# A combine of expert results with a gather buffer for every row set and a scale ahead, and one norm, summed by token tile, in the place of two

## The chip, the cores and the metric

One Trainium2 chip, one of its cores. The metric is the device time of one execution of the kernel in microseconds (us), the median of several runs. "The clock" is the granted clock of TensorE, as a share of 2.4 GHz.

## The reference

Two transformer blocks run one behind the other on 1024 tokens of 1024 features, all in float32. The first ends in a mixture of experts: every token goes to two of 16 experts and gets the weighted sum of the two results, added to the residual stream h. Between the blocks stand two norms, one behind the other:

```python
def hierarchical_moe(...):
    ...
    out = jnp.einsum('nef,efd->nd', act, w_down)
...
        h = h + hierarchical_moe(rms_norm(h, norm_ffn_g[layer]), ...)
    return rms_norm(h, norm_final_g)
...
def rmsnorm(x, g):
    xf = x.astype(jnp.float32)
    y = xf * lax.rsqrt(jnp.mean(xf * xf, axis=-1, keepdims=True) + EPS)
    return y.astype(x.dtype) * g
```

The output of `rms_norm(h, norm_final_g)` is the second block's residual stream x; its first step is `rmsnorm(x, attn_norm_2)`, whose result is multiplied with the input projections of three mixers (gated linear attention, S5, RG-LRU). Behind them come the output projection and a convolutional feed-forward part.

## The kernel before, in words

The stream h lies in SBUF with the features on the partitions: `hT` is eight pages of 128 features x 1024 tokens (`Hp[t]`). `W` ("work" in the profile) is 37 more pages of this size (`Wp[t]`; the last eight are `Bp[t]`). PSUM is used as four slots of 128x1024 that go round: every PSUM result has a number from `take()`, lies in slot number % 4, and TensorE waits in `slot(n)` until the result four numbers before it has been read (`emptied`). `done(n)` is the count of `mm_done` at which result n is complete. Each engine's program is written out by hand, and the engines meet by semaphores; there is no planner. `link()` on DVE makes the next instruction wait for the one before.

The stretch that the change touches stands between the expert blocks and the second block's projections:

- **Gathers.** The expert results lie in DRAM (`y_slots`), one row of 1024 floats for each slot. For each of the eight token tiles (128 tokens) POOL issues two indirect DMAs (L525), one for each of a token's two experts, into four buffers `YG` that go round; from the third tile on it first waits until the tile two before has been added to h (`ysum_ready`).
- **Combine.** DVE multiplies the first row set by its weight (L1593), and adds the second one times its weight (L1595). TensorE transposes the sum, 128x128 eight times (L788). DVE adds that to the tile's 128 columns in all eight pages of `hT` (L1599), before it turns to the next tile.
- **Norm `n_fin1`** (gain norm_final) and **norm `n_att2`** (gain attn_norm). One norm is: ACT squares the eight pages (L964), DVE adds them up (L1233, seven additions), TensorE sums over partitions with eight products of one column (L630) so that each token's sum lies on a partition, ACT takes the root (L971), DVE the inverse (L1239) and lays it on diagonals (L1240), TensorE spreads these with a product by ones (L639), and DVE applies gain and inverse root to each page (L1251). The first norm writes `hT` itself; its application is interleaved with the second norm's squares and additions. The second norm writes `Bp`.
- **Behind it.** `first_pair` (L590) multiplies two projections at a time, page by page as they come from the second norm; the others follow as `column_tile` (L570). DVE prepares the S5 matrices, `s5_b` and `s5_c`, which POOL has loaded once h is complete (DVE L1609 to L1620), and then waits for ACT to move the first projection out of PSUM (L1110) before it starts the RG-LRU convolution (L1626). The S5 part (L1644 and on) is a loop of eight groups on DVE, POOL and TensorE.

Names in the profile: `ps` is PSUM, `cst` holds constants, gains, the identity and the ones matrix.

## Time and profile before

| | |
|---|---|
| time of three runs | 2861.59, 2864.77, 2866.13 us; median 2864.77 |
| the profiled execution's own time | 2861.46 us |
| its span, first to last instruction | 2859.6 us |
| mean granted clock | 0.917 |
| busy, TensorE (PE) / DVE / ACT / POOL | 2511.2 / 1079.4 / 572.5 / 680.8 us |

The profile is a page of one execution with a trace of its instructions behind it, which can be asked for views. PE is TensorE's matmul side and PEld its weight loads, DVE is VectorE, ACT ScalarE, POOL GpSimd. A line "L788 MATMUL" is what line 788 of the kernel issued. A timeline row has the start, the length, engine, line, operation, output<-input, shape and count, and in brackets how long the engine was idle before it and what released it. A float32 product appears as two matmul instructions, a transpose as one. A windows row has, for a stretch of the span, its length, the busy time of PE, PEld, DVE, ACT and POOL with the instructions in brackets (only PE where so asked), the granted clock, the DMA share and GB/s. Averages over the whole span say little here: the stretch of the change is some 100 us long and is read by itself.

### The profile page before, as it was taken

How to read it: one execution, taken by the hardware profiler on the slowest of the kernel's cores; microseconds unless marked ns; L12 is line 12 of the kernel's file. 1: busy time of each engine (PE TensorE's matmuls, PEld its weight loads, DVE VectorE, ACT ScalarE, POOL GpSimd, SP SyncE). 2: the span in 40 equal slices, each digit the busy share in tenths (PEclk: the TensorE clock that was granted, in tenths of full speed). 3: DMA queues.
4: the chain of work that ended last, by engine and by line, in shares of the span. 5: the costliest groups of instructions: out<-in, count | busy, mean ns of one | idle time of the engine just before them, and what ended most of it. 6: DMA issues, size and time to landing. Idle time of an engine off the chain costs nothing. (4 is left out here: it accounts for less than half of the span.)

```text
span 2859.6 us, 27595 instructions
## 1 busy us (share of the span) xinstructions
PE 2511.2 (88%) x11034; PEld 1824.4 (64%) x11034; DVE 1079.4 (38%) x1788; ACT 572.5 (20%) x758; POOL 680.8 (24%) x448
## 2 busy tenths in 40 slices
PE   5999999997974999972896665989989999999997
PEld 4888899997762444432342224675458888888885
DVE  6400244454322111125589992552142212222124
ACT  3101455665101111102210000220021101001011
POOL 2323443462202000001023331000003233232321
PEclk9999999998976999995898887866989999999998
DMA  3111222233125677223000000000111111111111
GB/s 134 45 52 37 64 66 79 78 104 129 37 96 198 264 269 311 90 89 106 23 30 22 15 15 15 8 8 8 37 45 46 43 59 41 48 52 44 52 33 70
DMA packets 72044, 211.90 MB, mean 74 GB/s; under 512 B 4912, under 2 KB 36656, under 8 KB 68976
## 3 DMA queue, kind: packets, MB, share of 16 engines
q1 hardware_dynamic: 55712, 141.19, 14.3%
q0 software_dynamic: 11744, 52.70, 5.3%
q10 hardware_dynamic: 4464, 16.25, 1.4%
q8 instruction: 91, 1.49, 0.2%
q14 instruction: 33, 0.27, 0.0%
HBM read 165.03 MB, written 45.09 MB: 73 GB/s over the span
## 5 line engine op out<-in xcount | busy, mean ns | idle before, releaser
L608 PE MATMUL ps<-work_part 128*128 128x512 f32 x1472 | 574.3, 390 | 9.0 <-POOL work_part L463 7.2
L610 PE MATMUL ps<-work_part 128*128 128x512 f32 x1472 | 573.5, 390 | 0.0
L609 PE MATMUL ps<-work_part 128*128 128x512 f32 x1120 | 436.3, 390 | 0.0
L461 POOL CAST work_part<-ring 128x1024 fp32r<-128x1024 f32 (+2 forms) x108 | 104.9, 971 | 1147.1 <-PE ps L610 644.1
L608 PEld LDWEIGHTS ps<-work_part 128*128 128x128 f32 x1472 | 276.7, 188 | 67.7 <-issue 8.4
L610 PEld LDWEIGHTS ps<-work_part 128*128 128x128 f32 x1472 | 276.6, 188 | 57.7
L570 PE MATMUL ps<-work,ring 128*128 128x512 f32 x640 | 278.1, 595 | 2.7 <-DVE work L1790 2.7
L463 POOL TENSOR_TENSOR work_part<-ring,work_part 128x1024 fp32r<-128x1024 f32 (+2 forms) x108 | 241.1, 2233 | 8.6
L609 PEld LDWEIGHTS ps<-work_part 128*128 128x128 f32 x1120 | 210.6, 188 | 43.8
L570 PEld LDWEIGHTS ps<-work,ring 128*128 128x128 f32 x640 | 122.0, 191 | 157.4 <-issue 153.1
L759 PE MATMUL ps<-work 128*128 x496 | 218.6, 594 | 0.7 <-SPq L414 0.4
L1435 DVE CUSTOM_DVE_ANT_0 hT<-ps,hT 128x1024 f32<-128x1024 f32 (+2 forms) x86 | 85.1, 991 | 337.7 <-PE ps L674 337.7
L692 PE MATMUL ps<-work,hT 128*128 128x64 f32 x1600 | 194.8, 272 | 1.8 <-DVE work L1446 1.5
L692 PEld LDWEIGHTS ps<-work,hT 128*128 128x128 f32 x1600 | 188.5, 192 | 3.8 <-issue 1.9
L1464 DVE TENSOR_TENSOR hT<-ps,hT 128x1024 f32<-128x1024 f32 x48 | 58.8, 1225 | 341.8 <-PE ps L610 239.2
L759 PEld LDWEIGHTS ps<-work 128*128 128x128 f32 x496 | 92.1, 191 | 105.3 <-issue 105.3
L609 PE MATMUL ps<-hT_part,work_part 128*128 128x512 f32 x352 | 136.9, 389 | 0.0
L674 PE MATMUL ps<-work_part 128*128 128x512 f32 (+1 forms) x448 | 125.0, 396 | 1.6 <-ACT work L1007 1.1
L630 PE MATMUL ps<-cst,work 128*128 128x1 f32 x224 | 43.4, 324 | 81.0 <-DVE work L1233 81.0
L775 PE MATMUL ps<-work 128*128 x248 | 111.6, 592 | 1.6 <-DVE work L1575 1.6
L964 ACT ACTIVATE work<-hT 128x1024 f32<-128x1024 f32 x48 | 50.4, 1058 | 306.2 <-DVE hT L1464 222.2
L1569 DVE TENSOR_TENSOR work<-ps,work 128x256 f32<-128x256 f32 x31 | 13.2, 425 | 243.6 <-ACT work L1071 243.6
(271 smaller groups left out, 3210.7 us busy)
## 6 DMA issues: line engine op xcount, KB each, us to landing
work<-w_moe SPq DMA_DIRECT2D x16, 3072.0 KB, 11.2
ring<-w_up_units SPq DMA_DIRECT2D x44, 512.0 KB, 3.2
ring<-w_in_units SPq DMA_DIRECT2D x42, 512.0 KB, 3.3
x_slots<-hT SPq DMA_DIRECT2D x31, 512.0 KB, 3.5
work<-x_slots POOLq DMA_DIRECT2D x31, 512.0 KB, 4.3
y_slots<-work ACTq DMA_DIRECT2D x31, 512.0 KB, 2.6
ring<-w_down_units SPq DMA_DIRECT2D x24, 384.0 KB, 3.1
ring<-w_out_units SPq DMA_DIRECT2D x16, 512.0 KB, 3.3
```

The lines of the kernel that those rows point to most:

```text
L461: pool.tensor_copy(WHI[n % 2][:, 0:cols], w).then_inc(whi_ready, 1)
L463: pool.tensor_tensor(WLO[n % 2][:, 0:cols], w, WHI_F[n % 2][:, 0:cols], ALU.subtract).then_inc(wlo_ready, 1)
L570: mm = pe.matmul(ps[:, half * HALF:(half + 1) * HALF], w[:, k * P:(k + 1) * P], rhs[k][:, half * HALF:(half + 1) * HALF], start=(k == 0), ...
L608: pe.matmul(ps[:, c], whi[:, w], hi[k][:, c], start=(k == 0), stop=False)
L609: pe.matmul(ps[:, c], whi[:, w], lo[k][:, c], start=False, stop=False)
L610: mm = pe.matmul(ps[:, c], wlo[:, w], hi[k][:, c], start=False, stop=(k == len(hi) - 1))
L674: mm = pe.matmul(ps[:, b * HALF:b * HALF + w], QS[h % 2][:, i * P:(i + 1) * P], part[h % 2][:, c0:c0 + w], start=(part is KH), stop=(part ...
L692: mm = pe.matmul(ps[:, 0:DH], PT[u % 2][:, j * P:(j + 1) * P], Wp[16 + k0 + j][:, h * DH:(h + 1) * DH], start=(j == 0), stop=(j == k1 - k0 ...
L759: mm = pe.matmul(ps[:, 0:HALF], XT[b % 2][:, k * P:(k + 1) * P], xw[:, bass.ds(pages[b] + k * HALF, HALF)], start=(k == 0), stop=(k == NT ...
L775: mm = pe.matmul(ps[:, half * HALF:(half + 1) * HALF], HAT[b % 2][:, f * P:(f + 1) * P], xw[:, bass.ds(pages[b] + 4 * S + f * S + half * H ...
L1435: dve.tensor_tensor_reduce(out=banks(SB[u % 3][:, 0:nk]), in0=scores, in1=banks(bias), scale=-1.0, scalar=3.0e38, op0=ALU.add, op1=ALU.min ...
L1464: dve.tensor_tensor(Hp[m], PS[(n0 + m) % SLOTS][:, :], Hp[m], ALU.add).then_inc(h_ready, 1)
```

## The change

The gathers get a buffer each (16 pages, `YG`), so POOL issues all 16 without a wait. On DVE the scale and add of a tile (`ysum`) are issued ahead of the addition to h of the tile before (`ysum_to_h`). Both norms are replaced: as soon as a tile of h is complete, ACT squares its columns in all eight pages (`TSQ`, L1115), and TensorE multiplies them, 128x128 by two columns eight times (`P_TSUM`, L809), one column of ones and one of the squares of norm_final's gain (`gain_sums`). That gives for each token the sum of h^2 and the sum of (gain h)^2, from which both norms' roots follow: the combined norm's inverse root is 1/sqrt(S + EPS (V + EPS)), with V the mean of h^2 and S that of (gain h)^2. DVE puts both inverse roots on diagonals (`TDIAG`); TensorE spreads the combined one (`P_BOTH`) and then the first norm's (`P_FIRST`), both ahead of the projections (L816). DVE writes `Bp` = h x both gains x combined root (L1659, `hn_ready`) and behind it the new h = h x norm_final x first root (L1663, `hres_ready`), which is needed only where the second block's output projection is added to it.

The matmuls of the combine on TensorE before, in the order of issue, from the transposes to the projections:

```order
L788 MATMUL ps<-cst,work 128x128 x64
L630 MATMUL ps<-cst,work 128x1 x8
L639 MATMUL ps<-work,cst 128x512 x2
L630 MATMUL ps<-cst,work 128x1 x8
L639 MATMUL ps<-work,cst 128x512 x2
L590 MATMUL ps<-work,ring 128x512 x32
L570 MATMUL ps<-work,ring 128x512 x16
```

The same place in the change (L803 transposes, L809 sums, L816 spreads, L603 and L583 projections; the pair of L803 and L809 stands there for every tile):

```order
L803 MATMUL ps<-cst,work 128x128 x16
L809 MATMUL ps<-small,work 128x2 x8
L803 MATMUL ps<-cst,work 128x128 x8
...
L809 MATMUL ps<-small,work 128x2 x16
L816 MATMUL ps<-work,cst 128x512 x4
L603 MATMUL ps<-work,ring 128x512 x32
L583 MATMUL ps<-work,ring 128x512 x16
```

The sums have moved between the transposes, one tile behind them, and there are eight sets in the place of two; both spreads stand together ahead of the projections.

DVE before, from a tile of the combine to the S5 preparation:

```order
L1593 TENSOR_SCALAR work<-work 128x1024
L1595 SCALAR_TENSOR_TENSOR work<-work 128x1024
L1599 TENSOR_TENSOR hT<-ps,hT 128x8x128
L1233 TENSOR_TENSOR work<-work 128x1024 x7
L1239 RECIPROCAL std<-std 128x8
L1240 TENSOR_TENSOR work<-std,cst 128x1024
L1251 SCALAR_TENSOR_TENSOR hT<-hT,cst,ps 128x1024 x3
...
L1251 SCALAR_TENSOR_TENSOR work<-hT,cst,ps 128x1024 x8
L1609 TENSOR_SCALAR work<-work,s5p 128x128
```

And in the change:

```order
L1630 TENSOR_SCALAR work<-work 128x1024
L1631 SCALAR_TENSOR_TENSOR work<-work 128x1024
...
L1637 TENSOR_TENSOR hT<-ps,hT 128x8x128 x2
L1318 TENSOR_SCALAR small<-small 128x8
L1316 TENSOR_SCALAR small<-small 128x8
L1648 SCALAR_TENSOR_TENSOR small<-small 128x8
L1651 RECIPROCAL small<-small 128x16
L1653 TENSOR_TENSOR work<-small,cst 128x1024 x2
L1659 SCALAR_TENSOR_TENSOR work<-hT,small,ps 128x1024 x8
L1663 SCALAR_TENSOR_TENSOR hT<-hT,cst,ps 128x1024 x8
L1671 TENSOR_SCALAR work<-work,s5p 128x128
```

The fourteen additions of squares are gone from DVE, and the eight operations that write h stand now between the normed pages and the S5 preparation, where before they stood ahead of both.

The diff:

```diff
--- before.py
+++ after.py
@@ -130,3 +130,3 @@
         y_stored = [sem(f"y_stored{i}") for i in range(3)]
-        y_gathered = [sem(f"y_gathered{i}") for i in range(4)]
+        y_gathered = [sem(f"y_gathered{i}") for i in range(NT)]
         member_ready, rank_read, dispatch_ready, xtm_ready = (
@@ -136,2 +136,5 @@
         ysum_added = sem("ysum_added")
+        gains_ready, tsq_ready, tsum_taken, tvar_ready, troot_ready, tdiag_ready, hn_ready, hres_ready = (
+            sem("gains_ready"), sem("tsq_ready"), sem("tsum_taken"), sem("tvar_ready"), sem("troot_ready"),
+            sem("tdiag_ready"), sem("hn_ready"), sem("hres_ready"))
         out_stored = sem("out_stored")
@@ -257,5 +260,9 @@
                     of[t - lag] = take(1)
-        P_YSUM = take(8)
-        n_fin1 = add_norm(Hp, "norm_final", Hp, Wp[22:25], 8, take(2))
-        n_att2 = add_norm(Hp, "attn_norm", Bp, Wp[22:25], 8, take(2))
+        P_YSUM, P_TSUM = {}, {}
+        for tt in range(NT + 1):
+            if tt < NT:
+                P_YSUM[tt] = take(1)
+            if tt >= 1:
+                P_TSUM[tt - 1] = take(1)
+        P_BOTH, P_FIRST = take(1), take(1)
 
@@ -313,2 +320,3 @@
             emptied[use_f[i]] = (f_ready, i + 1)
+        emptied[P_BOTH], emptied[P_FIRST] = (hn_ready, NT), (hres_ready, NT)
         emptied[P_ROUTE], emptied[P_RANK] = (gdiff_ready, 1), (rank_read, 1)
@@ -320,3 +328,4 @@
             emptied[P_XTM + m] = (xtm_ready, m + 1)
-            emptied[P_YSUM + m] = (ysum_ready, m + 1)
+            emptied[P_YSUM[m]] = (ysum_ready, m + 1)
+            emptied[P_TSUM[m]] = (tsum_taken, m + 1)
             emptied[P_OUT2 + m] = (h_ready, 8 + m + 1)
@@ -391,3 +400,9 @@
         xw = W[:, 13:13 + XBUF * XPG, :].rearrange("p a b -> p (a b)")
-        YG = [Wp[13 + i] for i in range(4)]
+        YG = [Wp[13 + i] for i in range(2 * NT)]
+        TSQ = [Wp[2], Wp[3]]
+        TDIAG = [Wp[23], Wp[24]]
+        gain_sums = small[:, 0:2, :]
+        both_gains = small[:, 2, :]
+        tsums = small[:, 4:6, :]
+        troots = small[:, 6:8, :]
 
@@ -521,7 +536,5 @@
                 for r, name in enumerate(("p1i", "p2i")):
-                    k = (2 * tt + r) % 4
-                    if tt >= 2:
-                        pool.wait_ge(ysum_ready, tt - 1)
-                    pool.indirect_dma_start(YG[k], None, y_slots, bass.IndirectOffsetOnAxis(ap=R(name)[:, tt:tt + 1].bitcast(u32), axis=0),
-                                            bounds_check=NBLK * P - 1, oob_is_err=True).then_inc(y_gathered[k], 16)
+                    pool.indirect_dma_start(YG[2 * tt + r], None, y_slots,
+                                            bass.IndirectOffsetOnAxis(ap=R(name)[:, tt:tt + 1].bitcast(u32), axis=0),
+                                            bounds_check=NBLK * P - 1, oob_is_err=True).then_inc(y_gathered[tt], 16)
             pool.wait_ge(ysum_ready, NT)
@@ -783,10 +796,24 @@
 
-            for tt in range(NT):
-                pe.wait_ge(ysum_added, tt + 1)
-                ps = slot(P_YSUM + tt)
-                for k in range(NT):
-                    mm = pe.transpose(ps[:, k * P:(k + 1) * P], YG[(2 * tt + 1) % 4][:, k * P:(k + 1) * P], ident)
+            pe.wait_ge(gains_ready, 2)
+            for t in range(NT + 1):
+                if t < NT:
+                    pe.wait_ge(ysum_added, t + 1)
+                    ps = slot(P_YSUM[t])
+                    for k in range(NT):
+                        mm = pe.transpose(ps[:, k * P:(k + 1) * P], YG[2 * t + 1][:, k * P:(k + 1) * P], ident)
+                    mm.then_inc(mm_done, 1)
+                if t >= 1:
+                    pe.wait_ge(tsq_ready, t)
+                    ps = slot(P_TSUM[t - 1])
+                    for k in range(NT):
+                        mm = pe.matmul(ps[:, 0:2], TSQ[(t - 1) % 2][:, k * P:(k + 1) * P], gain_sums[:, :, k],
+                                       start=(k == 0), stop=(k == NT - 1))
+                    mm.then_inc(mm_done, 1)
+            for i, n in enumerate((P_BOTH, P_FIRST)):
+                pe.wait_ge(tdiag_ready, i + 1)
+                ps = slot(n)
+                for half in range(2):
+                    mm = pe.matmul(ps[:, half * HALF:(half + 1) * HALF], ones, TDIAG[i][:, half * HALF:(half + 1) * HALF],
+                                   start=True, stop=True)
                 mm.then_inc(mm_done, 1)
-            norm(n_fin1)
-            norm(n_att2)
 
@@ -811,3 +838,3 @@
 
-            first_pair(U_IN2, MAIN[0], MAIN[1], Bp, xn_ready, n_att2["xn0"])
+            first_pair(U_IN2, MAIN[0], MAIN[1], Bp, hn_ready, 0)
             main[0] = 2
@@ -1081,10 +1108,16 @@
 
-            def moe_gate(t):
-                act.wait_ge(ysum_ready, NT)
-            norm(n_fin1, moe_gate)
-
-            def fin1_gate(t):
-                act.wait_ge(xn_ready, n_fin1["xn0"] + t + 1)
-            norm(n_att2, fin1_gate)
-            act.wait_ge(normed, n_att2["index"] + 1)
+            act.activation(root_of_eps[:, 2 * NT - 1:2 * NT], epsc[:], ACT.Sqrt)
+            for t in range(NT + 1):
+                if t < NT:
+                    act.wait_ge(ysum_ready, t + 1)
+                    if t >= 2:
+                        act.wait_ge(mm_done, done(P_TSUM[t - 2]))
+                    act.activation(TSQ[t % 2].rearrange("p (k n) -> p k n", n=P), hT[:, :, t * P:(t + 1) * P],
+                                   ACT.Square).then_inc(tsq_ready, 1)
+                if t >= 1:
+                    act.wait_ge(mm_done, done(P_TSUM[t - 1]))
+                    act.activation(tsums[:, :, t - 1], PS[P_TSUM[t - 1] % SLOTS][:, 0:2], ACT.Copy).then_inc(tsum_taken, 1)
+            act.wait_ge(tvar_ready, 1)
+            act.activation(troots, tsums, ACT.Sqrt).then_inc(troot_ready, 1)
+            act.wait_ge(hn_ready, NT)
 
@@ -1588,16 +1621,45 @@
 
-            for tt in range(NT):
-                k = (2 * tt) % 4
-                a, b = YG[k], YG[k + 1]
-                dve.wait_ge(y_gathered[k], 16 * (tt // 2 + 1))
-                link(dve.tensor_scalar(a, a, R("w1")[:, tt:tt + 1], None, ALU.mult))
-                dve.wait_ge(y_gathered[k + 1], 16 * (tt // 2 + 1))
-                dve.scalar_tensor_tensor(out=b, in0=b, scalar=R("w2")[:, tt:tt + 1], in1=a, op0=ALU.mult,
+            dve.memset(gain_sums[:, 0, :], 1.0).then_inc(gains_ready, 1)
+            dve.tensor_tensor(both_gains, par("norm_final", 0, NT), par("attn_norm", 0, NT), ALU.mult)
+            dve.tensor_tensor(gain_sums[:, 1, :], par("norm_final", 0, NT), par("norm_final", 0, NT),
+                              ALU.mult).then_inc(gains_ready, 1)
+
+            def ysum(t):
+                a, b = YG[2 * t], YG[2 * t + 1]
+                dve.wait_ge(y_gathered[t], 32)
+                link(dve.tensor_scalar(a, a, R("w1")[:, t:t + 1], None, ALU.mult))
+                dve.scalar_tensor_tensor(out=b, in0=b, scalar=R("w2")[:, t:t + 1], in1=a, op0=ALU.mult,
                                          op1=ALU.add).then_inc(ysum_added, 1)
-                dve.wait_ge(mm_done, done(P_YSUM + tt))
-                cols = hT[:, :, tt * P:(tt + 1) * P]
-                dve.tensor_tensor(cols, PS[(P_YSUM + tt) % SLOTS][:, :].rearrange("p (k n) -> p k n", n=P), cols,
+
+            def ysum_to_h(t):
+                dve.wait_ge(mm_done, done(P_YSUM[t]))
+                cols = hT[:, :, t * P:(t + 1) * P]
+                dve.tensor_tensor(cols, PS[P_YSUM[t] % SLOTS][:, :].rearrange("p (k n) -> p k n", n=P), cols,
                                   ALU.add).then_inc(ysum_ready, 1)
-            norm(n_fin1, then=n_att2)
-            norm(n_att2, 6)
+
+            for t in range(NT + 1):
+                if t < NT:
+                    ysum(t)
+                if t >= 1:
+                    ysum_to_h(t - 1)
+            dve.wait_ge(tsum_taken, NT)
+            ts(tsums[:, 0, :], tsums[:, 0, :], 1.0 / D, EPS, ALU.mult, ALU.add)
+            ts(tsums[:, 1, :], tsums[:, 1, :], 1.0 / D, None, ALU.mult)
+            dve.scalar_tensor_tensor(out=tsums[:, 1, :], in0=tsums[:, 0, :], scalar=EPS, in1=tsums[:, 1, :],
+                                     op0=ALU.mult, op1=ALU.add).then_inc(tvar_ready, 1)
+            dve.wait_ge(troot_ready, 1)
+            link(dve.reciprocal(troots, troots))
+            for i in range(2):
+                dve.tensor_tensor(TDIAG[i].rearrange("p (t n) -> p t n", n=P),
+                                  troots[:, 1 - i, :].unsqueeze(2).to_broadcast([P, NT, P]),
+                                  ident.unsqueeze(1).to_broadcast([P, NT, P]), ALU.mult).then_inc(tdiag_ready, 1)
+            dve.wait_ge(ysum_ready, NT)
+            dve.wait_ge(mm_done, done(P_BOTH))
+            for k in range(NT):
+                dve.scalar_tensor_tensor(out=Bp[k], in0=Hp[k], scalar=both_gains[:, k:k + 1], in1=PS[P_BOTH % SLOTS][:, :],
+                                         op0=ALU.mult, op1=ALU.mult).then_inc(hn_ready, 1)
+            dve.wait_ge(mm_done, done(P_FIRST))
+            for k in range(NT):
+                dve.scalar_tensor_tensor(out=Hp[k], in0=Hp[k], scalar=par("norm_final", k), in1=PS[P_FIRST % SLOTS][:, :],
+                                         op0=ALU.mult, op1=ALU.mult).then_inc(hres_ready, 1)
 
@@ -1790,2 +1852,3 @@
                 dve.tensor_tensor(Bp[h], Bp[h], Wp[PG_G + h], ALU.mult).then_inc(gla_ready, 1)
+            dve.wait_ge(hres_ready, NT)
             add_to_h(P_OUT2, 8, n_mlp)
```

## Rows read from the trace of the kernel before

**Rows 1.** The page: the span of the profiled execution.

```profile
span 2859.6 us, 27595 instructions
```

**Rows 2.** Timeline, combine: start, length, engine, line, operation, idle and releaser.

```profile
1274.62 1.09 POOL L525 DMA_INDIRECT work<-y_slots,work  x1 [53.14 <-DMA y_slots<-work]
...
1278.94 0.75 DVE L1593 TENSOR_SCALAR work<-work 128x1024 f32<-128x1024 f32 x1 [7.76 <-DMA work<-y_slots,work]
1281.36 1.28 DVE L1595 SCALAR_TENSOR_TENSOR work<-work 128x1024 f32<-128x1024 f32 x1 [1.66 <-DMA work<-y_slots,work]
1282.70 1.97 PE L788 MATMUL ps<-cst,work 128*128 128x128 f32 x8 [12.88 <-DVE work L1595]
1284.70 1.22 DVE L1599 TENSOR_TENSOR hT<-ps,hT 128x1024 f32<-128x1024 f32 x1 [2.06 <-PE ps L788]
```

**Rows 3.** Timeline, first norm, from its squares to its sums, root, spread and application.

```profile
1327.38 2.95 ACT L964 ACTIVATE work<-hT 128x1024 f32<-128x1024 f32 x3 [66.12 <-DVE hT L1599]
...
1338.77 3.55 PE L630 MATMUL ps<-cst,work 128*128 128x1 f32 x16 [12.68 <-DVE work L1233]
1342.35 0.27 ACT L971 ACTIVATE std<-ps,epsc 128x8 f32<-128x8 f32 x1 [3.72 <-PE ps L630]
1342.65 0.20 DVE L1239 RECIPROCAL std<-std 128x8 f32<-128x8 f32 x1 [4.03 <-ACT std L971]
...
1344.17 3.70 PE L639 MATMUL ps<-work,cst 128*128 128x512 f32 x4 [1.85 <-DVE work L1240]
1347.91 3.66 DVE L1251 SCALAR_TENSOR_TENSOR hT<-hT,cst,ps 128x1024 f32<-128x1024 f32 x3 [3.80 <-PE ps L639]
```

**Rows 4.** Timeline, second norm and the first matmuls behind it.

```profile
1365.84 3.54 PE L630 MATMUL ps<-cst,work 128*128 128x1 f32 x16 [17.97 <-DVE work L1233]
...
1375.06 9.62 DVE L1251 SCALAR_TENSOR_TENSOR work<-hT,cst,ps 128x1024 f32<-128x1024 f32 x8 [3.87 <-PE ps L639]
...
1376.49 27.70 PE L590 MATMUL ps<-work,ring 128*128 128x512 f32 x64 [1.47 <-DVE work L1251]
```

**Rows 5.** Waits of DVE from 1376 to 1745: total us, times, longest.

```profile
DVE work L1626 <- ACT work L1110: 11.0, 1, 11.0
DVE work L1638 <- ACT work L1121: 10.7, 1, 10.7
DVE work L1644 <- ACT work L1125: 8.9, 1, 8.9
```

**Rows 6.** Timeline, DVE behind the second norm.

```profile
1384.83 0.29 DVE L1609 TENSOR_SCALAR work<-work,s5p 128x128 f32<-128x128 f32 x1
...
1403.63 0.81 DVE L1626 TENSOR_SCALAR work<-work,cst 128x1024 f32<-128x1024 f32 x1 [11.04 <-ACT work L1110]
```

**Rows 7.** Windows, S5 loop: length, busy (PE, PEld, DVE, ACT, POOL), clock, DMA, GB/s.

```profile
1460.00:1744.00 284.00, 184.79 (x395) 74.03 (x393) 266.50 (x412) 12.51 (x12) 111.70 (x47) 0.84 0.05 17
```

**Rows 8.** Groups of PE instructions from 830 to 870 us, by form.

```profile
L727 PE MATMUL ps<-cst,work 128*128 128x20 f32 x128 | 27.5, 381 | 9.8 <-DVEq L1263 9.8
```

**Rows 9.** Windows: routing product, transposes, same later, combine.

```profile
832.00:859.00 27.00, 27.00 (x128) 27.00 (x129) 0.00 (x0) 0.00 (x0) 0.00 (x0) 0.50 0.31 118
859.50:862.80 3.30, 3.30 (x17) 3.30 (x16) 2.82 (x16) 0.23 (x1) 0.00 (x0) 0.50 0.00 0
863.20:864.20 1.00, 1.00 (x11) 1.00 (x10) 0.83 (x6) 0.00 (x0) 0.00 (x0) 1.00 0.00 0
1282.00:1327.00 45.00, 15.75 (x64) 12.55 (x64) 23.89 (x23) 0.00 (x0) 12.06 (x12) 0.50 0.48 150
```

**Rows 10.** Timeline, PE: eight transposes, and 16 sum matmuls, at the full clock.

```profile
921.97 1.04 PE L750 MATMUL ps<-cst,work 128*128 128x128 f32 x8
...
1801.50 1.95 PE L630 MATMUL ps<-cst,work 128*128 128x1 f32 x16
```

**Rows 11.** DMA issues, 1270 to 1330 us: count, median us to landing.

```profile
work<-y_slots,work POOLq DMA_INDIRECT x16, 5.1
```

**Rows 12.** Windows: the first four gathers in flight.

```profile
1277.50:1282.00 4.50, 0.00 (x0) 0.00 (x0) 1.39 (x2) 0.00 (x0) 2.01 (x2) 0.50 0.95 321
```

## The prediction

> **What bounds it now.** All times below are microseconds from the start of one profiled execution, whose span is 2859.6 [rows 1] and whose own time is 2861.46; the median of the three timed runs is 2864.77, 3.3 more. I subtract from the profiled execution and carry the difference over to the median.
>
> I read the timeline of the changed stretch first. In the combine every token tile is one chain through three engines: the gathers land, DVE scales (0.75) and adds (1.28), PE turns the sum (1.97), DVE adds it to h (1.22), and only that last step lets POOL issue a gather for the tile two further on [rows 2]. Nothing overlaps but DVE's next scale. The first chain's second gather has landed at 1281.4, the last h is written when ACT, which has waited 66.1 for all eight, starts its squares at 1327.38 [rows 3]. Then two norms run one behind the other. The first has its sums on PE at 1342.3 (1338.77 + 3.55), and its application starts at 1347.91 [rows 3]. The second is interleaved with it, has its sums at 1369.4 and is applied from 1375.06. PE starts the next projection at 1376.49 [rows 4]. So the path here is a chain of handoffs, and PE is hardly used.
>
> I then asked what is behind it. From 1376 to 1745 DVE waits only three times, 11.0, 10.7 and 8.9, each time for an ACT result of a projection [rows 5]; the first of these ends at 1403.63, 27.1 behind PE's start at 1376.49 [rows 4, 6]. In the S5 loop DVE is busy 266.5 of 284 us while PE has 184.8 [rows 7]. This region is a DVE chain that starts when the projection starts. If the projection starts earlier, it moves as a whole, provided DVE is free in time. I forecast that the gain reaches the end undiminished.
>
> **The sum: the combine.** The 16 gathers now go out without any wait for buffers. Scale and add of tile t+1 are moved ahead of the addition of tile t to h. PE gets, for each tile, eight matmuls with two columns, Y before T: T(t-1) stands behind the transposes Y(t). In the profile each such matmul appears as two instructions, 16 a tile. No row of before has two columns; bounds are the one-column sums, 3.55 for 16 [rows 3], and the 20-column routing product, 27.5/128 x 16 = 3.44 [rows 8]. I take 3.55: it costs the same whatever the width, so it is the 128x128 operand that is paid for. Squares of one tile on ACT cost 0.98 (2.95 for three, [rows 3]), with the handoff 1.1, and hide under the T before.
>
> Per tile PE now has 1.97 + 3.55 = 5.52, DVE 0.75 + 1.28 + 1.22 = 3.25. The first four gathers moved 321 GB/s at a DMA share of 0.95 [rows 12]; a gather is 128 rows of 4 KB, 0.524 MB, so 1.63 each, 3.27 a tile (an estimate from that row). PE becomes the bound of the loop. Step by step: both gathers of tile 0 landed 1281.4; scale and add to 1283.5; Y0 to 1285.5. DVE does tile 1 to 1285.6, PE Y1 to 1287.6; meanwhile h0 to 1286.9 and its squares to 1288.0. T0 runs to 1291.6. Six pairs Y, T of 5.52 bring T6 to 1324.7, and T7 ends at 1328.2. The first norm's sums stood at 1342.3: **14.1 earlier**, although PE's work per tile has nearly tripled.
>
> **The sum: one norm for two.** From sums to application took 5.6 (1342.3 to 1347.9, [rows 3]). Now ACT copies two columns (0.27, the row of L971), DVE does three tiny operations (0.2 each, the row of L1239), ACT takes both roots in one go (inside the 5.6): 5.6 + 1.0 = 6.6, so the application of the combined gain starts at 1334.8 instead of 1375.06 [rows 4]. That is **26.2 more**, 40.3 in all: the whole second norm with its eight squares, seven additions, sums and spread is gone.
>
> **What is added on the path.** PE must also spread the first norm's root before the projection. Four instructions cost 3.70 at the low clock [rows 3], or 4 x 27.70/64 = 1.73 at the high one [rows 4]. It begins as the first spread ends (1334.8), so it is done at 1336.5 or 1338.5; the first application ends at 1336.1 beside it. Before, the projection began 1.43 after the application, now 1.7 to 3.7. I take 1337.0, nearest the high clock, because the granted clock had been raised when the spread before the projection was over (PE runs the projection at 0.433 an instruction from its start [rows 4]). Net: 1376.5 - 1337.0 = **39.5**.
>
> **What is covered, and by what.** The memset and two 8-column products on DVE lie in its 7.76 wait for the first gather [rows 2]. ACT's table for the root is loaded while it waits for the gathers. The s5 loads of POOL still follow the last h (now about 1322). The eight operations that write the normed h itself, 9.6 by the row of 1375.06 [rows 4], now stand on DVE before the S5 preparation. DVE: 1334.8 + 9.6 + 9.6 + 7.8 (the preparation, 1384.83 to 1392.59, [rows 6]) = 1361.8. Its next work can start at 1337.0 + 27.1 = 1364.1. The cover is the wait of 11.0, and about 2 of it is left; without it the overrun would be paid one for one. The PSUM buffer with the first norm's root is free at 1354.0; PE wants it back only behind the third projection, after 1364.
>
> **Time.** 2861.46 - 39.5 = 2822.0 for the profiled execution, 2864.77 - 39.5 = **2825.3** for the median.
>
> **Clock, rival 1: PE warms up in the combine.** In the combine the granted clock is 0.50 (1.2 GHz) with PE busy 15.75 of 45 [rows 9]. In 27 us of nothing but the 20-column product it stayed at 0.50; the transposes that followed ran 3.3 us at 0.50 and then at 1.00 [rows 9]. So narrow matmuls back to back do not raise it and back-to-back transposes do. In the new loop transposes are 1.97 of 5.52, 36%, as now (35%), and the rest is narrow, so I expect 0.50. Against that, Y0 and Y1 stand nearly together, and it may rise for a tile or two. If it rose and stayed at 2.4 GHz, Y costs 1.04 and T 1.95 [rows 10], 2.99 a tile, and the gathers' 3.27 bound: tile 7 landed at 1304.3, then scale and add 2.1, Y 1.04, h 1.3, squares 1.1, T 1.95 give 1311.8, 16.4 earlier: 2808.9. Chance 0.10.
> The Trainium skill, "TensorE: Matmul & The Clock Gate", Part 4, ("PE-mode transpose"), says that transposes do not count as activity for the full clock; by that rule this rival would have no chance. The trace speaks against the rule: nothing but transposes ran ahead of that rise.
>
> **Rival 2: the gathers get in each other's way (the other side of zero).** Without a wait for a buffer, 16 gathers lie on one queue. For it: so far at most four did. Against: those four overlapped at 321 GB/s. Paces up to (1317.3 - 1281.4)/14 = 2.6 a gather cost nothing, since PE wants tile 7 only at 1319.4. If they ran one by one at their 5.1 from issue to landing [rows 11], plus an issue of 1.1 [rows 2], the last would land at 1274.6 + 16 x 6.2 = 1373.8; behind it come 10.1 (scale and add 2.1, Y 2.0, h 1.3, squares 1.1, T 3.6), 6.6 to the application and 2.2 to the projection: 1392.7, 16.2 later than now, 2881. It turns into a loss above 5.2 each, since (1376.5 - 8.8 - 10.1 - 1274.6)/16 = 5.2. Chance 0.05: 0.02 a loss, 0.01 nothing, 0.02 a smaller gain.
>
> **Rival 3: DVE is late after the norm.** If the cover of 2 is not there and DVE's eight operations stand on the path, up to 9.6 are given back: 2835. For it: only 2 are left. Against: all its pieces are measured. Chance 0.05.
>
> **Rival 4: the gain is swallowed later**, by something that does not start from the projection. Then about 2865. Against: in [rows 5] DVE waits for nothing else. Chance 0.02.
>
> **How the numbers follow.** Forecast 0.78. Range: down to rival 1 and the spread of medians (some 3), 2806; up to a cold second spread, two or three unforeseen handoffs and most of rival 3, 2834. A measurement here can tell about 0.2% (5.7 us) from no change. Faster: 0.78 + 0.10 (rival 1) + 0.02 (of rival 2) + 0.05 (rival 3) + 0.01 (a rival 4 that swallows only part) = 0.96; same: 0.01 of rival 2 and 0.01 of rival 4 = 0.02; slower: 0.02 of rival 2.
>
> **What would show it.** In the profile after: the T instructions in groups of about 3.5 with PE hardly idle from 1288 to 1328; granted clock 0.50 there; gathers all issued by about 1297; the application of both gains about 40 earlier, at 1335; the projection at 1337; DVE's wait for the first projection down from 11.0 to about 2. I am wrong on the mechanism if PE waits for DVE inside the loop (then gathers or DVE bind), if T costs much less than 3.5, or if DVE has no wait left before its convolution.

## The result and the profile after

The changed kernel takes 2822.1 us, the median of four runs (2818.02 to 2822.66), where the kernel before takes 2865.45 beside it (2861.59 to 2867.38). The ratio is 0.9847, with a 95% interval of 0.983 to 0.9864. It is 43.3 us faster by the medians; the forecast was 2825.3, 39.5 faster.

From the page of the kernel after, whose profiled execution took 2822.43 us: the span, and the busy time of the engines.

```profile
span 2820.6 us, 27756 instructions
...
PE 2531.7 (90%) x11130; PEld 1848.3 (66%) x11130; DVE 1062.7 (38%) x1779; ACT 564.7 (20%) x756; POOL 683.0 (24%) x448
```

PE has 20.5 more to do than before and the program ends 39.0 earlier (the spans): none of the gain is work saved on the busiest engine. The timeline of the stretch, all engines, with the columns of [rows 2]: the gathers, the loop of transposes (Y, L803) and sums (T, L809; T0 is that of tile 0), the norm, the projection, and DVE's first work for the next part.

```profile
1277.73 1.09 POOL L537 DMA_INDIRECT work<-y_slots,work  x1 [53.15 <-DMA y_slots<-work]
...
1286.53 1.94 PE L803 MATMUL ps<-cst,work 128*128 128x128 f32 x8 [13.62 <-issue]
...
1289.87 1.97 PE L803 MATMUL ps<-cst,work 128*128 128x128 f32 x8 [1.40 <-DVE work L1631]
...
1292.09 3.57 PE L809 MATMUL ps<-small,work 128*128 128x2 f32 x16 [0.25 <-ACT work L1115]
...
1295.52 1.95 PE L803 MATMUL ps<-cst,work 128*128 128x128 f32 x8
...
1297.26 3.41 PE L809 MATMUL ps<-small,work 128*128 128x2 f32 x16
...
1300.53 1.95 PE L803 MATMUL ps<-cst,work 128*128 128x128 f32 x8
...
1322.33 6.83 PE L809 MATMUL ps<-small,work 128*128 128x2 f32 x32
...
1329.19 0.17 ACT L1119 ACTIVATE small<-ps 128x2 f32<-128x2 f32 x1 [3.24 <-PE ps L809]
...
1331.83 5.73 PE L816 MATMUL ps<-work,cst 128*128 128x512 f32 x8 [2.67 <-DVE work L1653]
...
1335.71 9.62 DVE L1659 SCALAR_TENSOR_TENSOR work<-hT,small,ps 128x1024 f32<-128x1024 f32 x8 [2.81 <-PE ps L816]
...
1337.39 27.63 PE L603 MATMUL ps<-work,ring 128*128 128x512 f32 x64
...
1364.46 0.81 DVE L1688 TENSOR_SCALAR work<-work,cst 128x1024 f32<-128x1024 f32 x1 [1.93 <-ACT work L1143]
```

I measure the stretch from the first gather to the start of the projection (L590 before, L603 now), since both ends are rows. It was 1376.49 - 1274.62 = 101.87 [rows 2, 4] and is 1337.39 - 1277.73 = 59.66: **42.2 less**. The first gather itself stands 3.1 later here, although nothing ahead of it was changed; over the kernels of this study it stands anywhere from 1273.18 to 1280.21, which is why I measure from it. Cut where the sums over all tiles are done (1342.32 before, 1329.16 now), the gain is 16.3 ahead of that point and 25.9 behind it. The first gather's start varies because of what runs ahead of it, and that is not explained here. From the projection to the end of the span it was 2859.6 - 1376.49 = 1483.1 and is 2820.6 - 1337.39 = 1483.2. So the whole gain is made between these two rows, and nothing gives it back.

Windows of the loop: length, busy time (PE, PEld, DVE, ACT, POOL), clock, DMA share, GB/s.

```profile
1286.00:1292.00 6.00, 3.91 (x16) 3.13 (x16) 4.62 (x6) 1.02 (x1) 5.09 (x4) 0.50 0.96 376
1292.00:1329.00 37.00, 36.91 (x176) 36.91 (x176) 19.14 (x18) 8.64 (x15) 8.92 (x9) 0.50 0.42 148
```

From 1292 on PE is busy for 36.91 of 37 us. In the combine before it was busy for 15.75 of 45 [rows 9]. That is the change of regime: a chain of handoffs has become a stream that one engine bounds. The clock stays at 0.50 all the same.

Waits of DVE from 1337 to 1710, after (before: [rows 5]): total us, times, longest.

```profile
DVE work L1700 <- ACT work L1154: 10.7, 1, 10.7
DVE work L1706 <- ACT work L1158: 8.9, 1, 8.9
DVE work L1688 <- ACT work L1143: 1.9, 1, 1.9
```

The first of these three waits, for the first projection, was 11.0 and is 1.9; the other two are what they were. These are the two bounds behind the change, and they moved with the projection.

### The profile page after: what moved, and what is told of

The parts are those of the page before. It is cut to its first block and busy times, and to the rows that moved or that the text cites. A ratio compares the mean times of both kernels' runs of the same rounds, so it can differ in the third digit from the quotient of the medians.

```text
span 2820.6 us, 27756 instructions
## 1 busy us (share of the span) xinstructions
PE 2531.7 (90%) x11130; PEld 1848.3 (66%) x11130; DVE 1062.7 (38%) x1779; ACT 564.7 (20%) x756; POOL 683.0 (24%) x448
## 3 DMA queue, kind: packets, MB, share of 16 engines
q1 hardware_dynamic: 55712, 141.19, 14.4%
## 5 line engine op out<-in xcount | busy, mean ns | idle before, releaser
L583 PE MATMUL ps<-work,ring 128*128 128x512 f32 x640 | 278.1, 595 | 2.7 <-DVE work L1852 2.7
L583 PEld LDWEIGHTS ps<-work,ring 128*128 128x128 f32 x640 | 122.0, 191 | 157.5 <-issue 153.2
L1049 ACT ACTIVATE hT<-ps 128x1024 f32<-128x1024 f32 (+2 forms) x128 | 104.7, 818 | 0.0
L1237 ACT ACTIVATE work<-ps,cst 128x1024 f32<-128x1024 f32 x22 | 26.6, 1207 | 382.2 <-PE ps L623 373.3
```

Of the source, the lines that this page charges most:

```text
L583: mm = pe.matmul(ps[:, half * HALF:(half + 1) * HALF], w[:, k * P:(k + 1) * P], rhs[k][:, half * HALF:(half + 1) * HALF], start=(k == 0), ...
L1049: act.activation(PT[u % 2][:, 0:(k1 - k0) * P], PS[n % SLOTS][:, 0:(k1 - k0) * P], ACT.Copy).then_inc(pT_ready, 1)
```

## The experiments

Each is compared with the kernel before that ran beside it on the same chip (medians 2863.2 to 2865.2). "F to P" is the time from the first gather to the projection in its profiled execution: 101.87 before, 59.66 after. Line numbers differ by a few between kernels; the names of the operations do not. Against the change I compare medians (its own is 2822.1) and F to P. The medians of the kernel before differ by up to 2.2 between the sets in which these runs were taken, the runs of one kernel by 1 to 6, and the experiments ran on three chips; so a difference of two or three us between medians says little, and there F to P decides. F to P holds one term that moves by itself: from the application of the new norm to the projection it is 1.4 to 2.7 in the eleven kernels that have the new norm, by when the clock rises in the spreads (1.68 in the change).

### Part 1: the buffers alone

The kernel before, with 16 gather buffers in place of four:

```diff
-        YG = [Wp[13 + i] for i in range(4)]
+        YG = [Wp[13 + i] for i in range(2 * NT)]
...
-                    k = (2 * tt + r) % 4
-                    if tt >= 2:
-                        pool.wait_ge(ysum_ready, tt - 1)
+                    k = 2 * tt + r
```

> The kernel before with 16 gather buffers and nothing else. Theory (the chain of a tile bounds the old combine, not the gathers): only the waits of L1595 for the second gather of every other tile go, 1.54 + 1.51 + 1.35 = 4.4 us, so the kernel is 4 to 5 us faster than before. Rival (POOL's waits for buffers, 24.8 us in all, are what the change recovers): 10 us or more faster.

Measured: 2859.8, 4.9 faster; ratio 0.9984 (0.9975 to 0.9994). As expected. Behind the first tile DVE no longer waits for a gather, and each tile costs 5.27 (5.35 and 5.30 for the first two): scale, add, handoff, transposes, handoff, addition to h, one behind the other.

### Part 2: the buffers and the scale ahead, with the old norms

The DVE loop of the kernel before is turned around as in the change:

```diff
-            for tt in range(NT):
+            def scale_add(tt):
...
+            def add_h(tt):
                 dve.wait_ge(mm_done, done(P_YSUM + tt))
...
+            for tt in range(NT + 1):
+                if tt < NT:
+                    scale_add(tt)
+                if tt >= 1:
+                    add_h(tt - 1)
             norm(n_fin1, then=n_att2)
```

> The kernel before with 16 buffers and the scale ahead; both norms as before. Theory: the loop is bound by DVE's 0.75 + 1.28 + 1.22 = 3.25 a tile, so the last h is written 26 + 2 us after 1281.4 instead of 46 us after it: 18 us faster than before. Rival (16 gathers in flight get slower than 3.3 a tile): 12 us faster or less.

Measured: 2844.65, 20.0 faster; ratio 0.9931 (0.9914 to 0.9947). F to P is 83.22, 18.65 less. As expected. From the timeline of this kernel, two additions to h (L1599) and ACT's start:

```profile
1301.68 1.22 DVE L1599 TENSOR_TENSOR hT<-ps,hT 128x1024 f32<-128x1024 f32 x1
...
1304.79 1.22 DVE L1599 TENSOR_TENSOR hT<-ps,hT 128x1024 f32<-128x1024 f32 x1
...
1308.19 2.95 ACT L962 ACTIVATE work<-hT 128x1024 f32<-128x1024 f32 x3 [47.41 <-DVE hT L1599]
```

With PE doing nothing but the transposes, DVE is the bound: 3.1 a tile, and ACT's first squares for the old norm start at 1308.19, 34.0 behind the first gather (52.76 before, [rows 2, 3]). The two norms behind it take what they took: 49.2 from there to the projection at 1357.37, and 49.1 before [rows 3, 4].

### Part 3: the norm alone

The kernel after, with the four buffers of before and no scale ahead:

```diff
+                if tt >= 2:
+                    pool.wait_ge(ysum_ready, tt - 1)
                 for r, name in enumerate(("p1i", "p2i")):
-                    pool.indirect_dma_start(YG[2 * tt + r], None, y_slots,
+                    pool.indirect_dma_start(YG[2 * (tt % 2) + r], None, y_slots,
...
-            for t in range(NT + 1):
-                if t < NT:
-                    ysum(t)
-                if t >= 1:
-                    ysum_to_h(t - 1)
+            for t in range(NT):
+                ysum(t)
+                ysum_to_h(t)
```

> The changed kernel with the old combine: four buffers, POOL's waits, no scale ahead; only the norm is the new one. Theory (the sums by token tile fit into the gaps of the old chain, and both parts' gains overlap): the last h as late as before, then 6.8 for two sets of sums, 6.6 and 1.7: projection 35.4 earlier than before, so 35 us faster than before and 7 us slower than the change. Rival (the gain of the change is mostly in the combine): less than 25 us faster than before.

Measured: 2833.45, 31.2 faster; ratio 0.9892 (0.9875 to 0.9908). F to P is 70.49. It misses by 4: 35 were expected. Three Y rows of its PE timeline (the last one ends with the window that was asked for):

```profile
1301.46 1.97 PE L805 MATMUL ps<-cst,work 128*128 128x128 f32 x8 [2.10 <-DVE work L1633]
...
1307.56 1.97 PE L805 MATMUL ps<-cst,work 128*128 128x128 f32 x8 [0.93 <-DVE work L1633]
...
1314.76 1.54 PE L805 MATMUL ps<-cst,work 128*128 128x128 f32 x6 [2.02 <-DVE work L1633]
```

The pitch, the distance between the starts of two Y, alternates between 6.0 to 6.1 and 7.2 to 7.3; in the kernel before (all Y rows of its timeline) it alternates between 5.3 and 6.7 to 6.8. The change has one wait for both gathers of a tile (`wait_ge(y_gathered, 32)`), where before DVE scaled the first row set while the second still came. So the same kernel again with a wait for each gather:

```diff
-                dve.wait_ge(y_gathered[t % 2], 32 * (t // 2 + 1))
+                dve.wait_ge(y_gathered[2 * (t % 2)], 16 * (t // 2 + 1))
                 link(dve.tensor_scalar(a, a, R("w1")[:, t:t + 1], None, ALU.mult))
+                dve.wait_ge(y_gathered[2 * (t % 2) + 1], 16 * (t // 2 + 1))
```

> The new norm on the old combine, as in the run before on it, but DVE waits for each of a tile's two gathers where it needs it, as the kernel before does. Theory (31 instead of 35 us were gained there because the scale now stands idle until both gathers have landed, 0.6 to 1.9 us a tile): 3 to 4 us faster than with the single wait, 35 us faster than before. Rival (the shortfall is PE's sums in the chain of a tile): no difference between the two.

Measured: 2828.6, 36.6 faster; ratio 0.9873 (0.9856 to 0.9889). F to P is 67.82. Its pitch lies between 5.3 and 6.7, as 5.5 from 1296.75 to 1302.25 and 6.5 to 1308.76. From the second Y to the last it takes 36.8, where the kernel before takes 36.1 and the one with a single wait 39.8. It is 4.9 faster than with one wait by the medians and 2.7 by F to P, where the expectation had 3 to 4: the single wait made most of the shortfall, and the sums in PE's queue add 0.7 to the old loop. The two parts by themselves give 18.65 and 101.87 - 67.82 = 34.05, together 52.7, and the change has 42.2 of it. The gains overlap because each part lifts a different bound of one loop: with the old norm DVE's 3.1 a tile is left, with the sums in the loop PE's 5.0. Six times that difference is 11.4; the 52.7 and the 42.2 differ by 10.5. No run has one norm for two without the sums in the loop, so these two halves of the new norm are not told apart by an experiment. Looked at the other way, the order of DVE and the buffers are worth 18.65 alone and 59.66 against 67.82, so 8.2, beside the new norm.

### Part 4: what the scale ahead is worth, and on what it depends

The kernel after with its 16 buffers, but each tile's addition to h ahead of the next tile's scale (the second half of the diff of part 3):

> The changed kernel with 16 buffers, but each tile's addition to h before the next tile's scale. Theory (PE's transposes and sums, 5.0 a tile, bound the new loop): the chain of a tile is 5.3, so 7 x 0.3 = 2 us slower than the change. Rival (the scale ahead carries the gain): 2 a tile, 10 us slower or more.

Measured: 2825.44, 39.2 faster; ratio 0.986 (0.9844 to 0.9877), 3.3 slower than the change. F to P is 63.70, 4.0 more. Of these 3.0 lie ahead of the end of the last sums: the pitch is 5.27 (DVE's chain) instead of 5.01 (PE's work), and T0 starts 1.6 later behind the first gather. The other 1.0 is the later rise of the clock in the spreads. Near the 2 expected, and far from the rival's 10: DVE's chain and PE's work per tile happen to be nearly equal.

Then the scale ahead with four buffers (the first half of that diff alone):

> The changed kernel with four gather buffers as before, POOL waiting for the tile two before; scale still ahead. From h of a tile to the landing of the second gather it allows are 7.5 us (1285.9 to 1293.4 in the trace of before), then 2.1 for scale and add, 2.0 and 1.2 to the next h: 12.9 for two tiles, 6.4 a tile against 5.0. Theory: 8 us slower than the change. Rival (PE's sums hide the gathers anyway): no difference.

Measured: 2852.07, only 11.1 faster; ratio 0.9962 (0.9948 to 0.9976). That is 30 slower than the change where I had expected 8, the widest miss of the study. F to P is 93.67, 34.0 more. Its timeline, two tiles of it (L539 the gathers, L1632 and L1633 scale and add, L1639 the addition to h, L805 Y, L811 T):

```profile
1289.58 1.00 POOL L539 DMA_INDIRECT work<-y_slots,work  x1 [8.65 <-DVE hT L1639]
...
1296.28 0.75 DVE L1632 TENSOR_SCALAR work<-work 128x1024 f32<-128x1024 f32 x1 [7.47 <-DMA work<-y_slots,work]
...
1298.27 1.22 DVE L1639 TENSOR_TENSOR hT<-ps,hT 128x1024 f32<-128x1024 f32 x1
...
1298.41 1.97 PE L805 MATMUL ps<-cst,work 128*128 128x128 f32 x8 [4.88 <-DVE work L1633]
...
1300.26 1.00 POOL L539 DMA_INDIRECT work<-y_slots,work  x1 [8.36 <-DVE hT L1639]
...
1309.00 1.97 PE L805 MATMUL ps<-cst,work 128*128 128x128 f32 x8 [4.80 <-DVE work L1633]
```

A tile now costs 10.6 (Y at 1298.41 and 1309.00). Read it from DVE: its queue is scale(t), add(t), h(t-1). Scale(t) waits 7.47 for its gather; h(t-1), which needs nothing but PE's long finished Y, stands behind it; and POOL may issue gather t+1 only after h(t-1). At 1298.27 DVE does h, and only at 1300.26 and a little later the two gathers of one more tile go out. Only one tile is ever in flight, and its whole latency is on the path. With four buffers the scale ahead is a loss of 18.6 by the medians (2833.45 without it, in part 3) and 23.2 by F to P, where with sixteen it is a gain of 3.3: neither the buffers nor the order can be judged without the other. What I had left out is what stands behind the wait in DVE's queue. If so, one more tile of buffers must cure it:

```diff
-        YG = [Wp[13 + i] for i in range(4)]
+        YG = [Wp[13 + i] for i in range(6)]
...
-                if tt >= 2:
-                    pool.wait_ge(ysum_ready, tt - 1)
+                if tt >= 3:
+                    pool.wait_ge(ysum_ready, tt - 2)
```

> The changed kernel with six gather buffers (three tiles) that go round, POOL waiting for the tile three before, scale ahead. Theory (with four, DVE waits for a gather that POOL may only issue after an addition to h which stands behind that very wait, 10.6 us a tile; with six that addition stands ahead of it): from an h to the end of the scale three tiles on are 7.5 + 2.1 us, three tiles last 15: within 2 us of the change. Rival (each buffer fewer costs in proportion): 15 us slower or more.

Measured: 2825.06, 40.1 faster; ratio 0.9858 (0.9841 to 0.9874), 3 slower than the change, where 2 at most were expected; F to P is 62.76, also 3.1 more. Two buffers give back 27 of the 30. DVE's waits from 1288 to 1330:

```profile
DVE work L1632 <- DMA work<-y_slots,work: 14.5, 4, 4.8
```

It still waits four times, but PE, with its longer queue of work, feels little of it: from the start of T0 to that of T6 it takes 32.5 (1291.75 to 1324.27), where the change takes 30.2 (1292.09 to 1322.33). Of the 16 buffers ten are worth 3 us here.

### Part 5: the size of the sums

The forecast made T the largest term of the loop. In the change it is a float32 product, issued as two instructions for each 128x128 block. Here squares and gain factors are written as fp32r, for which one instruction does; this rounds the squares and the factors:

```diff
-        TSQ = [Wp[2], Wp[3]]
+        TSQ = [Wr[2][:, :], Wr[3][:, :]]
...
-        gain_sums = small[:, 0:2, :]
+        gain_sums = Wr[5][:, 0:2 * NT].rearrange("p (a b) -> p a b", a=2)
...
-            dve.memset(gain_sums[:, 0, :], 1.0).then_inc(gains_ready, 1)
+            dve.tensor_scalar(gain_sums[:, 0, :], par("norm_final", 0, NT), 0.0, 1.0, ALU.mult, ALU.add).then_inc(gains_ready, 1)
```

> The changed kernel with squares and gains written as fp32r, so that each product of the sums is one instruction instead of two. Theory (PE bounds the new loop): PE falls to 1.6 + 0.9 to 1.7 a tile, below DVE's 3.25, which then bounds; T7 ends 14 to 15 us earlier: 13 to 15 us faster than the change. Rival (DVE or the gathers bind the loop already): 2 us faster at most.

Measured: 2808.15 (2807.1 to 2808.66), 55.1 faster than before, ratio 0.9805 (0.9789 to 0.9822), and 14 faster than the change by the medians. F to P is 46.32, 13.3 less than the change's. From its timeline, PE, one tile and the next Y:

```profile
1296.62 1.97 PE L803 MATMUL ps<-cst,work 128*128 128x128 f32 x8
1298.24 1.85 PE L809 MATMUL ps<-work_part 128*128 128x2 f32 x8
1299.95 1.97 PE L803 MATMUL ps<-cst,work 128*128 128x128 f32 x8
```

T is eight instructions of 1.85 together, and the pitch is 3.33. The window of its loop, columns as above:

```profile
1292.00:1312.00 20.00, 20.00 (x98) 20.00 (x98) 17.44 (x18) 6.71 (x12) 7.04 (x6) 0.50 0.61 215
```

The time came out as expected, the bound did not: DVE was expected to bind with 3.25 a tile, but PE needs 3.33, the upper end of what it was given, and is full, while DVE is busy for 17.44 of 20. Both now have about the same work per tile. This is the fastest kernel of the study.

### Part 6: DVE's cover

The forecast called the wait of 11.0 the cover of DVE's added 9.6, with 2 left. To take it away, the eight operations of L1663, which write h, are issued once more into pages that nobody reads, 9.6 us:

```diff
             for k in range(NT):
+                last = dve.scalar_tensor_tensor(out=Wp[(19, 20, 21, 22, 25, 26, 23, 24)[k]], in0=Hp[k], scalar=par("norm_final", k),
+                                                in1=PS[P_FIRST % SLOTS][:, :], op0=ALU.mult, op1=ALU.mult)
+            link(last)
+            for k in range(NT):
```

> The changed kernel with the eight operations that write h through the first norm done once more, into pages nobody reads: 9.6 us more on DVE behind the norm. Theory (1.9 us of cover are left, and what goes over it reaches the end): 7.7 us slower than the change. Rival (DVE is covered there, the projection bounds): no difference.

Measured: 2821.06, ratio 0.9851 (0.9835 to 0.9867), the time of the change itself. A miss: 7.7 were expected and none came. DVE began the convolution without a wait at 1370.45, 34.1 behind the projection (at 1336.32) where it is 27.1 in the change, so 7 later as foreseen. The wait behind it, for the second ACT result:

```profile
DVE work L1704 <- ACT work L1154: 3.7, 1, 3.7
```

It was 10.7 [rows 5] and is 3.7: it took the delay. And on PE the matmuls that read DVE's convolution (L847):

```profile
1377.52 7.03 PE L847 MATMUL ps<-work,cst 128*128 128x512 f32 x16
```

They follow the third projection (L583) without idle time, 41.2 behind the start of the projections as in the change (1337.39 to 1378.59). So the convolution is wanted not when the first projection is there, but when PE has done the third one. I read DVE's first wait as the cover, and the cover reaches on to the first engine that waits for DVE. To find its end, the same with 16 operations, 19.2 us:

```diff
             dve.wait_ge(mm_done, done(P_FIRST))
+            for again in range(2):
+                for k in range(NT):
+                    last = dve.scalar_tensor_tensor(out=Wp[(19, 20, 21, 22, 25, 26, 23, 24)[k]], in0=Hp[k], scalar=par("norm_final", k),
+                                                    in1=PS[P_FIRST % SLOTS][:, :], op0=ALU.mult, op1=ALU.mult)
+                link(last)
```

> The changed kernel with the eight operations that write h done three times: 19.2 us more on DVE. With them doubled nothing was lost; DVE's two waits behind the norm had been 1.9 and 10.7 us and 3.7 of the second was left. Theory (these two waits are one cover of about 13 us, because the third projection on PE has to be over before the gates are computed): 19.2 - 9.0 - 3.7 = 6 to 7 us slower than the change. Rival (nothing of this stretch of DVE reaches the end, since the S5 loop takes it up): no difference.

Measured: 2831.15 (2830.06 to 2832.51), ratio 0.9884 (0.9868 to 0.9901): 9.0 slower than the change, where 6 to 7 were expected. DVE's wait for the second ACT result:

```profile
DVE work L1705 <- ACT work L1154: 4.4, 1, 4.4
```

And from its timeline of PE, the matmuls that read the convolution, with two windows of PE (length, busy, clock, DMA share, GB/s):

```profile
1382.31 10.03 PE L847 MATMUL ps<-work,cst 128*128 128x512 f32 x16 [6.88 <-DVE work L1695]
```

```profile
1375.50:1382.30 6.80, 0.00 (x0) 0.68 0.25 77
1382.30:1388.00 5.70, 5.70 (x7) 0.50 0.00 0
```

PE now waits 6.88 for DVE's convolution. While it is idle the granted clock falls, and the first of its 16 matmuls there run at 0.50: they take 10.03 instead of 7.03, busy without a gap. From the first projection to L855 it is 71.85 where the change has 61.80, so 10.05 are lost of 19.2: 7.05 ahead of these matmuls and 3.0 in them. With the clock up PE would have had to wait again, for the second convolution, which ends at 1386.9, about 1.1 behind the first half of L847; so some 1.9 of the 3.0 are what the clock took (an estimate from these rows). From the projection to the end of the span it is 11.6 more than in the change.

The waits of DVE do not add up to a cover, as that expectation had it: 4.4 of the second one are left, because the ACT result that it waits for stands behind PE's gate products and came later itself. What counts is PE. By the rows of the change the second convolution ends at 1373.9, and PE would take it up halfway through L847 (1378.59 + 3.5 = 1382.1); with DVE's own wait of 1.9 that is a cover of about 10 (an estimate from these rows). By the same reckoning 1.1 of it are left in the run with 9.6 more (the second convolution ends at 1379.9, PE wants it at 1381.0), and nothing was lost there. So the cover that the change leaves is about 10 us, not 2, and what goes over it brings the clock down besides.

### Part 7: the clock

Rival 1 had PE warm up in the combine. It did not, so the question is whether the loop would hold a full clock if it started with one. 14 products of 128x512 on constants are put ahead of the combine:

```diff
+        P_WARM = take(1)
...
             pe.wait_ge(gains_ready, 2)
+            ps = slot(P_WARM)
+            for i in range(14):
+                mm = pe.matmul(ps[:, 0:HALF], ones, mat("rg", 0, HALF), start=True, stop=True)
+            mm.then_inc(mm_done, 1)
```

> The changed kernel with 14 products of 128x512 on constants, read by nobody, while PE waits for the first gathers: TensorE enters the combine at the full clock. Theory (transposes and narrow sums cannot hold it): the clock falls to 0.50 within the first tiles, 0 to 3 us faster than the change. Rival (it holds once it is up): Y and T cost 1.0 and 1.9, DVE bounds, 14 us faster.

Measured: 2821.51, ratio 0.9855 (0.9838 to 0.9871), the time of the change. Windows of its PE start:

```profile
1280.00:1284.00 4.00, 4.00 (x14) 1.94 (x13) 2.04 (x2) 0.00 (x0) 3.39 (x3) 1.00 1.00 307
1284.00:1288.00 4.00, 1.11 (x8) 0.88 (x7) 2.97 (x3) 0.00 (x0) 3.08 (x4) 0.88 0.99 397
1288.00:1292.00 4.00, 3.74 (x19) 3.34 (x17) 3.96 (x5) 1.45 (x2) 3.08 (x4) 0.50 0.96 367
```

The clock is 1.00 at the first Y and 0.50 from the second on, but between them PE had been idle for 2.88 us, so this run says nothing on the loop. In the next one three more such products fill that gap:

```diff
                     mm.then_inc(mm_done, 1)
+                    if t == 0:
+                        for i in range(3):
+                            pe.matmul(PS[P_WARM % SLOTS][:, 0:HALF], ones, mat("rg", 0, HALF), start=True, stop=True)
```

> The changed kernel with the 14 products of 128x512 ahead of the combine and three more between the first and the second transposes, where the clock had fallen. Theory (a third of the time on transposes, the rest narrow sums, doesn't hold the full clock): the clock falls within the next two tiles, 0 to 3 us faster than the change. Rival (it holds): Y 1.0 and T 1.9, DVE's 3.1 bounds, 13 us faster.

Measured: 2818.68 (2818.22 to 2819.18), ratio 0.9841 (0.9824 to 0.9857), 3.4 faster than the change by the medians and 2.2 by F to P (57.50), where the rival had 13. Its PE timeline (L809 Y, L813 the filler, L818 T) and its windows:

```profile
1284.84 1.05 PE L809 MATMUL ps<-cst,work 128*128 128x128 f32 x8
1285.73 2.74 PE L813 MATMUL ps<-cst 128*128 128x512 f32 x6
1288.41 1.10 PE L809 MATMUL ps<-cst,work 128*128 128x128 f32 x8
1290.63 1.95 PE L818 MATMUL ps<-small,work 128*128 128x2 f32 x16 [1.13 <-ACT work L1124]
1292.44 1.08 PE L809 MATMUL ps<-cst,work 128*128 128x128 f32 x8
1293.75 3.09 PE L818 MATMUL ps<-small,work 128*128 128x2 f32 x16 [0.23 <-ACT work L1124]
1296.70 1.95 PE L809 MATMUL ps<-cst,work 128*128 128x128 f32 x8
```

```profile
1288.00:1292.00 4.00, 2.87 (x23) 2.23 (x21) 3.96 (x5) 1.06 (x1) 3.39 (x3) 1.00 0.95 354
1292.00:1296.00 4.00, 3.77 (x27) 3.53 (x27) 3.96 (x5) 1.37 (x3) 3.08 (x4) 0.79 0.87 291
1296.00:1300.00 4.00, 4.00 (x20) 4.00 (x21) 2.98 (x4) 1.04 (x3) 3.28 (x3) 0.50 0.95 342
```

Three tiles of transposes and one of sums ran at the full clock (Y 1.05 to 1.10, T 1.95), as in [rows 10]. The clock fell in the window from 1292, in which PE was busy 3.77 of 4, and with PE busy for every us from 1296 to 1320 it did not come back. What this leaves open: PE had been idle for 1.13 ahead of the first T, so the run doesn't tell whether the stream brought the clock down or that gap did. It does tell that this stream doesn't raise it once it is down, and that 17 products of filler buy only 2 to 3 us.

## Why the prediction was right, and where it was off

The net is 39.5 forecast, 42.2 measured from gather to projection: the forecast has 1337.0 - 1274.6 = 62.4 there, the trace 59.66. The mechanism is the forecast one, and the 2.7 between them are 1.0 worse, 3.1 better in the loop, and 0.6 better behind it. Up to the end of the sums the forecast gained 14.1 and the trace 16.3; from there to the projection it is 25.4 (26.2 less 0.8 for the added spread) and 25.9. By its steps:

- **T0's start.** Forecast 13.4 behind the first gather (1288.0 - 1274.6), measured 1292.09 - 1277.73 = 14.4. The second tile's gathers came later than the forecast had them: Y1 stands 3.3 behind Y0, not 2.1. 1.0 worse. POOL had issued the last gather at 1301.6, 23.9 behind the first; the forecast had it at about 1297, 22 behind.
- **The pair Y, T** was the mis-sized term. The forecast added the lengths of two rows, 1.97 + 3.55 = 5.52. Measured is a pitch of 5.01 (1295.52, 1300.53, and so on). The recorded length of a row reaches past the start of the next group: T starts 1.74 behind a Y of 1.95, and the next Y 3.27 behind a T of 3.41. Over six pairs that is 3.0 better. T7 ended 51.4 behind the first gather (1322.33 + 6.83), forecast 53.6.
- **Width does not matter**, the guess between the one-column sums of [rows 3] and the 20 columns of [rows 8], was right: 16 instructions take 3.41 in the stream. That the 128x128 operand is what is paid for fits the window of the loop, in which PEld, the weight loads, is busy for as long as PE (36.91 of 37).
- **PE is the bound of the loop**: right, 36.91 busy of 37, and shown by experiment: shortening T alone gave 14 us (part 5). The gathers do not bind (rival 2): without the wait for buffers they moved 376 GB/s from 1286 to 1292, not less than the 321 of [rows 12].
- **Sums to application**: forecast 6.6, measured 1335.71 - 1329.16 = 6.55 (1329.16 is the end of T7).
- **The added spread and the projection's start**: forecast 2.2 behind the application, with 1.7 and 3.7 as the ends; measured 1.68, where it was 1.43 before. So the added spread costs 0.25 here. The granted clock is 0.50 from 1333 to 1335 and 1.00 from 1336 to 1337.4, so it rose within the second spread, and more than half of that spread lies beside the first page's application, which the projection needs anyway. That 1.68 came out is partly luck: the kernels of parts 6 and 7 have the same instructions here and show 2.3, 2.6, 2.4 and 1.6.
- **DVE's place behind the norm**: its wait for the first projection was forecast at 2 and is 1.93. The size was right, but the claim beside it and rival 3 were wrong: "without it the overrun would be paid one for one". Part 6 shows that the next 9.6 cost nothing. The rival's price of 9.6 did not exist at that point; its mechanism does, from about 10 on. The forecast took DVE's own next wait for the end of the cover and did not look at which engine reads DVE's result, and when.
- **Rival 1, the clock**: it stayed at 0.50, as forecast. Where it was raised beforehand it fell again, but behind an idle gap of PE, so whether the stream alone would have held it stays open (part 7).
- **Rival 4**: from the projection to the end it is 1483.1 before and 1483.2 after, and 1482.8 to 1485.4 in every other kernel but the one with DVE's work tripled (1494.8).

By the medians the gain is 43.3; against 42.2 in the traces that is within what runs of one kernel differ.

Left open: PE and DVE now have 3.3 and 3.1 a tile with fp32r sums. Whether moving the scale to ACT would bring more was not tried, since PE would bind either way. Nor was the spread moved behind the first matmuls of the projection; at most 0.5 us lies there in the change, between the end of the first page's application (1335.71 + 1.2) and the projection, and up to 1.5 where the clock rises later.

## What to carry to other kernels

Before a wait for a refilled buffer is moved ahead of the operation that frees one, count the tiles that are still in flight with that operation queued behind the wait; with two tiles of buffers the reordering cost 19 to 23 us, with eight it gained 3.3, and three tiles were enough to come within 3 of that. A cover does not end at the first wait of the engine that gets more work: follow it to the first other engine that waits for its result. Where TensorE is that engine, the wait can cost its clock as well: behind an idle time of 6.9 its next matmuls ran at 0.50. The pitch of a stream of matmul groups is the distance of their starts in a trace, not the sum of their lengths.
